# The final norm of a recurrent-mixer and mixture-of-experts layer: all rows normed under the last expert's down product, that expert's rows normed again and written by index

## What is computed

```python
def rms_norm(x, g):
    y = x * lax.rsqrt(jnp.mean(x * x, axis=-1, keepdims=True) + EPS)
    return y * g

def expert_choice_ffn(h, w_router, w_gate, w_up, w_down):
    cap = CAPACITY_FACTOR * n // N_EXPERTS            # 128 rows per expert
    aff = softmax(h @ w_router)
    gate, idx = lax.top_k(swapaxes(aff, 1, 2), cap)   # each expert picks its rows
    xg = h[idx]
    hid = silu(xg @ w_gate) * (xg @ w_up)
    y = (hid @ w_down) * gate[..., None]
    return zeros.at[idx].add(y)

x = x + mod[:, 2] * y_lat
h = modulate(rms_norm(x, norm_ffn_g), mod[:, 3], mod[:, 4])
x = x + mod[:, 5] * expert_choice_ffn(h, ...)
return rms_norm(x, final_g)
```

## Time and profile before

| what | us |
|---|---|
| median of three runs | 1784.28 |
| the profiled execution's own time | 1784.54 |
| its span (first to last record) | 1782.4 |
| own time less span | 2.14 |
| PE busy / DVE busy / ACT busy / POOL busy | 1610.7 / 1391.7 / 1222.2 / 213.3 |

### The profile page before, as it was taken

One profiled execution on the slowest core, in us unless ns is written; L12 is line 12 of the kernel. 1 busy time (PEld: TensorE's weight loads), 2 busy tenths in 40 slices (PEclk: granted clock), 3 DMA queues, 4 the chain that ended last, 5 costly groups with the idle time before them and its releaser, 6 DMA issues.

```text
span 1782.4 us, 21010 instructions
## 1 busy us (share of the span) xinstructions
PE 1610.7 (90%) x7524; PEld 1321.7 (74%) x7524; DVE 1391.7 (78%) x1044; ACT 1222.2 (69%) x1138; POOL 213.3 (12%) x129
## 2 busy tenths in 40 slices
PE   4999999997896049999999999999999999999992
PEld 1777777776785038888888888888888888888872
DVE  2677887789312958998988988988988988988982
ACT  3688788875324138787787787787787778777752
POOL 0400000003000500101101101011011011011010
PEclk6999999998997569999999999999999999999996
DMA  9223433434566039999999999999999999999945
GB/s 347 80 92 122 154 112 124 155 106 131 201 231 282 0 122 372 361 405 381 374 405 377 378 401 369 388 393 371 401 381 371 402 378 368 402 386 365 397 176 212
DMA packets 106448, 511.25 MB, mean 287 GB/s; under 512 B 10362, under 2 KB 36632, under 8 KB 55200
## 3 DMA queue, kind: packets, MB, share of 16 engines
q1 hardware_dynamic: 98912, 483.33, 69.7%
q0 software_dynamic: 7488, 27.27, 5.6%
HBM read 479.10 MB, written 31.46 MB: 286 GB/s over the span
## 4 chain that ended last, share of the span: by engine, by line
PE 84%; DVE 9%; ACT 3%; SPq 2%; DMA 1%; issue 1%; POOL 0%; ACTq 0%; DVEq 0%; POOLq 0%
PE psum L1281 13%; PE psum L1283 13%; PE psum L1289 13%; PE psum L1333 7%; PE psum L1335 7%; PE psum L1340 7%; PE psum L1082 5%; PE psum L1084 5%; PE psum L1083 5%; PE psum L1320 2%; PE psum L1190 2%; PE psum L1191 2%; PE psum L1192 2%; SPq L276 1%; DVE top_id L994 1%; DVE top_val L992 1%
## 5 line engine op out<-in xcount | busy, mean ns | idle before, releaser
L1007 DVE TENSOR_TENSOR part_l<-raw,part_h 128x2048 fp32r<-128x2048 f32 x378 | 844.0, 2285 | 71.6 <-ACT part_h L517 70.1
L517 ACT ACTIVATE part_h<-raw 128x2048 fp32r<-128x2048 f32 x384 | 720.8, 1917 | 158.1 <-PE psum L1289 82.4
L1281 PE MATMUL psum<-part_h,xgT_h 128*128 128x512 f32 x1024 | 284.5, 395 | 4.6 <-DVE xgT_l L1032 4.6
L1283 PE MATMUL psum<-part_h,xgT_l 128*128 128x512 f32 x1024 | 280.0, 390 | 0.0
L1289 PE MATMUL psum<-part_l,xgT_h 128*128 128x512 f32 x1024 | 279.9, 390 | 0.0
L1283 PEld LDWEIGHTS psum<-part_h,xgT_l 128*128 128x128 f32 x1024 | 192.8, 188 | 40.8
L1289 PEld LDWEIGHTS psum<-part_l,xgT_h 128*128 128x128 f32 x1024 | 192.6, 188 | 40.7
L1281 PEld LDWEIGHTS psum<-part_h,xgT_h 128*128 128x128 f32 x1024 | 189.6, 189 | 41.7 <-DVE xgT_l L1032 5.0
L1333 PE MATMUL psum<-part_h,hidT_h 128*128 128x512 f32 x512 | 158.7, 391 | 1.4 <-DVE hidT_l L1019 1.4
L1335 PE MATMUL psum<-part_h,hidT_l 128*128 128x512 f32 x512 | 158.5, 391 | 0.0
L1340 PE MATMUL psum<-part_l,hidT_h 128*128 128x512 f32 x512 | 137.2, 390 | 0.0
(11 more groups left out here) (213 smaller groups left out, 2318.4 us busy)
## 6 DMA issues: line engine op xcount, KB each, us to landing
raw<-in_exp_w_gate_dram SPq DMA_DIRECT2D x128, 1024.0 KB, 6.7
raw<-in_exp_w_up_dram SPq DMA_DIRECT2D x128, 1024.0 KB, 6.3
raw<-in_exp_w_down_dram SPq DMA_DIRECT2D x128, 1024.0 KB, 8.7
ada_piece<-in_ada_w_dram SPq DMA_DIRECT2D x16, 1024.0 KB, 6.6
ada_buf<-in_ada_w_dram SPq DMA_DIRECT2D x8, 1024.0 KB, 12.9
u_raw<-in_a_w_in_dram SPq DMA_DIRECT2D x10, 512.0 KB, 3.8
g_raw<-in_a_w_in_dram SPq DMA_DIRECT2D x10, 512.0 KB, 8.6
y_scr<-y_h POOLq DMA_DIRECT2D x10, 512.0 KB, 3.8
```

Source lines behind the costliest of these rows:

```text
L517: return nc.scalar.activation(dst, src, ACT.Identity)
L1007: v.tensor_tensor(part_l[slot][:], raw[slot][:], part_h[high][:].bitcast(F32), ALU.subtract).then_inc(sem["part_l_ready"], 1)
L1281: mm(dst, xgT_h[slot][:, i, :], wh[:, f, :], start=(i == 0), stop=False)
L1283: mm(dst, xgT_l[slot][:, i, :], wh[:, f, :], start=False, stop=False)
```

## The change

All eight tiles of `x_scr` are loaded when the scatter of expert 14 (the last but one) has landed, into tiles `fin[t]` that lie in buffers free by then, tiles 3 to 7 also behind the use of up chunks u4 to u6 of the last expert. ACT squares them in three groups (tiles 0 to 2, 3 and 4, 5 to 7), the output of Square going to PSUM banks 0 to 3, with one Sqrt for a group, put between its splits: group 0 behind the split of d5, group 1 behind d6, group 2 behind d7. DVE scales group 0 in place between its splits of d6 and d7, groups 1 and 2 behind d7 and ahead of `expert_out(E - 1)`. SP stores each tile. `fin_g` is loaded behind the last weight chunk.

The last expert's scatter into `x_scr` is gone. Instead, POOL gathers its 128 rows of `x_scr` (with 15 experts added) into `x_last` (the buffer of `xg`) when scatter 14 has landed; at the end DVE adds them to `y_out`, ACT squares and takes the root, DVE takes the reciprocal and multiplies, and POOL writes the 128 rows to the output by index, once the stores of all eight tiles have landed.

```diff
@@ -158,10 +158,11 @@
     hidT_l = place("hidT_l", [P, FF // P, P], F32R, 184)
     y_out = place("y_out", [P, D], F32, 192)
 
-    fin_in = place("fin_in", [P, NT, D], F32, 0)
-    fin_out = place("fin_out", [P, NT, D], F32, 32)
-    fin_g = place("fin_g", [P, D], F32, 64)
-    fin_junk = place("fin_junk", [P, D], F32, 68)
+    fin_kb = [148, 152, 160] + [raw_kb[i // 2] + 4 * (i % 2) for i in range(NT - 3)]
+    fin = [place(f"fin{t}", [P, D], F32, kb) for t, kb in enumerate(fin_kb)]
+    fin_g = place("fin_g", [P, D], F32, 201)
+    x_last = xg
+
     assert base + (SM + 2.8125) * KB <= nc.sbuf_usable_end
 
     psum = nc.alloc_psum_tensor("psum", [P, 8, HALF], F32)
@@ -199,7 +200,7 @@
         id_ready first_id_ready gathered xg_turned xgT_ready xgT_h_ready xgT_l_ready part_h_ready part_l_ready
         chunk_used silu_done hid_ready hid_turned hidT_h_ready hidT_l_ready
         y_ready id2_ready scattered fin_g_loaded fin_sq fin_rms fin_rstd
-        fin_ready fin_stored bias_loaded""".split()
+        fin_ready fin_stored last_loaded last_step last_stored bias_loaded""".split()
     piece_loaded = [stack.enter_context(nc.semaphore(f"piece_loaded{i}")) for i in range(2)]
     raw_loaded = [stack.enter_context(nc.semaphore(f"raw_loaded{i}")) for i in range(NR)]
 
@@ -416,15 +417,15 @@
                 load_chunk(E - 1, "d", i)
 
 
-            sp.wait_ge(sem["chunk_used"], 3 * E * CHUNKS)
             sp.dma_start(fin_g[:], row_of(final_g)).then_inc(sem["fin_g_loaded"], 16)
-            sp.wait_ge(sem["scattered"], 16 * E)
+            sp.wait_ge(sem["scattered"], 16 * (E - 1))
             for t in range(NT):
-                sp.dma_start(fin_in[:, t, :], x_scr[t * P:(t + 1) * P, :]).then_inc(x_loaded[t], 16)
+                if t >= 3:
+                    sp.wait_ge(sem["chunk_used"], chunk(E - 1, "u", 4) + (t - 3) // 2 + 1)
+                sp.dma_start(fin[t][:], x_scr[t * P:(t + 1) * P, :]).then_inc(x_loaded[t], 16)
             for t in range(NT):
                 sp.wait_ge(sem["fin_ready"], t + 1)
-                sp.dma_start(out[0, t * P:(t + 1) * P, :], fin_out[:, t, :]).then_inc(sem["fin_stored"], 16)
-            sp.wait_ge(sem["fin_stored"], 16 * NT)
+                sp.dma_start(out[0, t * P:(t + 1) * P, :], fin[t][:]).then_inc(sem["fin_stored"], 16)
             for i in range(2):
                 sp.wait_ge(x2_stored[i], PER_SLOT)
                 sp.wait_ge(n_stored[i], PER_SLOT)
@@ -506,8 +507,15 @@
                 gather(e, sem["id_ready"], e)
                 scatter(e - 2, e - 1)
             scatter(E - 2, E - 1)
-            scatter(E - 1, E)
-            pool.wait_ge(sem["scattered"], 16 * E)
+            pool.wait_ge(sem["scattered"], 16 * (E - 1))
+            pool.wait_ge(sem["xg_turned"], 2 * E)
+            nc.gpsimd.indirect_dma_start(x_last[:], None, x_scr, bass.IndirectOffsetOnAxis(ap=id_gather[:, 0:1], axis=0)
+                                         ).then_inc(sem["last_loaded"], 16)
+            pool.wait_ge(sem["fin_stored"], 16 * NT)
+            pool.wait_ge(sem["last_step"], 4)
+            nc.gpsimd.indirect_dma_start(out[0], bass.IndirectOffsetOnAxis(ap=id_gather[:, 0:1], axis=0), y_out[:], None
+                                         ).then_inc(sem["last_stored"], 16)
+            pool.wait_ge(sem["last_stored"], 16)
             pool.wait_ge(sem["y_stored"], 32 * NB)
 
 
@@ -724,18 +732,34 @@
             with act.Fori(1, E // 2) as j:
                 expert(j * 2, 0)
                 expert(j * 2 + 1, 1)
+            groups_fin = ((0, 3), (3, 5), (5, NT))
+            junk_fin = [psum[:, 2 * s:2 * s + 2, :].rearrange("p b f -> p (b f)") for s in range(2)]
+
+            def squares(part):
+                lo, hi = groups_fin[part]
+                for t in range(lo, hi):
+                    act.wait_ge(x_loaded[t], 32)
+                    if t >= 2:
+                        act.wait_ge(sem["fin_sq"], t - 1)
+                    nc.scalar.activation(junk_fin[t % 2], fin[t][:], ACT.Square, accum_out=stat[:, 0, t:t + 1]).then_inc(sem["fin_sq"], 1)
+                act.wait_ge(sem["fin_sq"], hi)
+                nc.scalar.activation(stat[:, 1, lo:hi], stat[:, 0, lo:hi], ACT.Sqrt, scale=1.0 / D,
+                                     bias=eps[:]).then_inc(sem["fin_rms"], 1)
+
             for i in range(CHUNKS):
                 split(E - 1, "d", i)
                 if i == 4:
                     turn_hidden(E - 1)
-
-            act.wait_ge(sem["chunk_used"], 3 * E * CHUNKS)
-            for t in range(NT):
-                act.wait_ge(x_loaded[t], 32)
-                nc.scalar.activation(fin_junk[:], fin_in[:, t, :], ACT.Square, accum_out=stat[:, 0, t:t + 1]).then_inc(sem["fin_sq"], 1)
-                act.wait_ge(sem["fin_sq"], t + 1)
-                nc.scalar.activation(stat[:, 1, t:t + 1], stat[:, 0, t:t + 1], ACT.Sqrt, scale=1.0 / D,
-                                     bias=eps[:]).then_inc(sem["fin_rms"], 1)
+                elif i == 5:
+                    squares(0)
+                elif i == 6:
+                    squares(1)
+            squares(2)
+            act.wait_ge(sem["last_step"], 1)
+            nc.scalar.activation(junk_fin[0], y_out[:], ACT.Square, accum_out=stat[:, 0, NT:NT + 1]).then_inc(sem["fin_sq"], 1)
+            act.wait_ge(sem["fin_sq"], NT + 1)
+            nc.scalar.activation(stat[:, 1, NT:NT + 1], stat[:, 0, NT:NT + 1], ACT.Sqrt, scale=1.0 / D,
+                                 bias=eps[:]).then_inc(sem["last_step"], 1)
 
 
         @block.vector
@@ -1056,20 +1080,36 @@
             with dve.Fori(1, E // 2) as j:
                 expert(j * 2, 0)
                 expert(j * 2 + 1, 1)
+            groups_fin = ((0, 3), (3, 5), (5, NT))
+
+            def scaled(part):
+                lo, hi = groups_fin[part]
+                dve.wait_ge(sem["fin_rms"], part + 1)
+                v.reciprocal(stat[:, 0, lo:hi], stat[:, 1, lo:hi]).then_inc(sem["fin_rstd"], 1)
+                dve.wait_ge(sem["fin_rstd"], part + 1)
+                for t in range(lo, hi):
+                    v.scalar_tensor_tensor(fin[t][:], fin[t][:], stat[:, 0, t:t + 1], fin_g[:], ALU.mult, ALU.mult
+                                           ).then_inc(sem["fin_ready"], 1)
+
             for i in range(CHUNKS):
                 split(E - 1, "d", i)
                 if i == 4:
                     gate_up(E - 1)
                     turn_hidden(E - 1)
+                elif i == 6:
+                    dve.wait_ge(sem["fin_g_loaded"], 16)
+                    scaled(0)
+            scaled(1)
+            scaled(2)
             expert_out(E - 1)
-
-            dve.wait_ge(sem["fin_g_loaded"], 16)
-            for t in range(NT):
-                dve.wait_ge(sem["fin_rms"], t + 1)
-                v.reciprocal(stat[:, 0, t:t + 1], stat[:, 1, t:t + 1]).then_inc(sem["fin_rstd"], 1)
-                dve.wait_ge(sem["fin_rstd"], t + 1)
-                v.scalar_tensor_tensor(fin_out[:, t, :], fin_in[:, t, :], stat[:, 0, t:t + 1], fin_g[:], ALU.mult, ALU.mult
-                                       ).then_inc(sem["fin_ready"], 1)
+            dve.wait_ge(sem["y_ready"], 2 * E)
+            dve.wait_ge(sem["last_loaded"], 16)
+            v.tensor_tensor(y_out[:], y_out[:], x_last[:], ALU.add).then_inc(sem["last_step"], 1)
+            dve.wait_ge(sem["last_step"], 2)
+            v.reciprocal(stat[:, 0, NT:NT + 1], stat[:, 1, NT:NT + 1]).then_inc(sem["last_step"], 1)
+            dve.wait_ge(sem["last_step"], 3)
+            v.scalar_tensor_tensor(y_out[:], y_out[:], stat[:, 0, NT:NT + 1], fin_g[:], ALU.mult, ALU.mult
+                                   ).then_inc(sem["last_step"], 1)
 
 
         @block.tensor
```

## The result

Four runs of the changed kernel gave 1765.05 to 1766.59 us, median 1766.10, against 1784.99 for four runs of the kernel before: ratio 0.9893, 95% interval 0.988 to 0.9906. It is faster by 18.9 us. The forecast was a gain of 22.3 us and a time of 1762.0, within 1760.0 to 1765.5; the measured median lies 0.6 above the range. The direction was right, the size was not.

A forecast was written before the change was run, and what follows sets the result against it. PE bounds the kernel until 1749.50, followed by an uncovered tail: 31.45 us removed from 1750.95 on, 9.15 added, 22.3 saved, span 1760.1. Forecast median 1762.0 us, range 1760.0 to 1765.5.

The forecast's parts named there:

- To the span's end 0.3: Last term of the added tail: 0.3 us from the landing of the write by index to the span's end, at 1760.1.
- Cover: Under the last down product: squares and scaling fit in idle ACT and DVE; DVE ends at 1748.8, margin 0.7 us.
- POOL's start: In the tail, from DVE's last multiply to POOL's write: 0.2 us taken, with 0.1 to 0.8 kept as bounds.
- The write by index: Landing of POOL's final write: 4.2 us, taken from the indirect gather, between a plain store 2.6 and accumulating scatter 6.4.
- The gather of `x_last`: Behind scatter 14: issued about 1715.3, landed by 1727, read by DVE at 1751; no cost, 24 us of cover.
- starved gather of the shared-port rule: Rival: gather descriptors starve until DVE idles, at worst 1748.8, landing at 1753.0: 1764.2 us; chance 0.04.
- Table load: In ACT's group 0: one load of 1.28 us, none in the tail; the skill's figure would add 0.7 us.
- Stores: Tile stores at the end: last issued at 1748.8, no queue, landed at 1751.4, at 6.2 us landing by 1755.0.
- Their rival: The last stores, not the multiply, release the final write: 1762.6, or 1764.6 with a burst of five; chance 0.06.
- The slower rival: Squares wait on a late tile 2 ahead of ACT's split d6, stalling PE; chance 0.02, half of it slower.
- change of sign: In the slower rival: the gain turns to loss where tile 2 lands at 1759; at 1762 the time is 1787.
- the limit that this pricing sets: In the slower rival: ACT must start group 0, 5.0 us long, by 1737; every us later costs one more.

The follow-up runs named there:

- the changed kernel's second profile: The changed kernel run again unaltered, in a second group of four runs: median 1765.01 us, from 1764.41 to 1765.86.
- the kernel whose norm is not covered: Against the changed kernel, the eight tiles' squares and scaling moved behind the last down chunk, loads and write by index left in place: median 1776.04 us.
- the run with late loads: Against the changed kernel, SP holds back the eight tile loads until PE has used down chunk d2: median 1777.15 us.
- the two whose SP waits: The changed kernel with the wait for the last write moved from POOL to SP, median 1762.58 us; the same with the last rows' chain in halves, 1762.77.

## Why the prediction was wrong

The mechanism was right, and one term of its sum was mis-sized: the step **"To the span's end 0.3"**. I took that from the kernel before, where SP came last, and carried it over to an end at which POOL comes last. It measured 3.6, of which 3.18 is POOL's DRAIN. That DRAIN is the cause: one more wait on POOL brought 3.3 us of tail into the old kernel, and moving the last wait to SP took 1.8 us out of the new one. The row stood in the trace of before, at 1758.6, but the busy view leaves such instructions out, and none of the rows that the prediction works with shows it.

By the prediction's own steps, each in the profiled execution:

| step | forecast | measured |
|---|---|---|
| ACT: split d6 starts | 1731.4 | 1731.28 |
| DVE: group 2 ends | 1748.8 | 1747.90 |
| `y_out` starts | 1749.53 | 1749.53 |
| last multiply ends | 1755.4 | 1755.23 |
| POOL's write is issued | 1755.6 | 1756.03 |
| its landing takes | 4.2 | 3.4 |
| landing to the span's end | 0.3 | 3.6 |
| span | 1760.1 | 1763.0 |

- **Cover**: right. The squares into PSUM took 1.00 to 1.03, below the 1.04 of rows 6. One started 1.04 behind another; only the last of a group, with its Sqrt behind it, took 1.15 to 1.17. Three scalings took 3.67, not 3.85. The prediction misread one thing here without harm: it has ACT and DVE idle from 1730 on, but they still worked 3.65 and 2.29 us between 1730 and 1735 in the kernel before. Its own sum of the two queues does count those splits.
- **POOL's start**: 0.8 after DVE's multiply. I took only the 0.19 ahead of the DMA; the chain shows 0.54 "issue" before that, and the old kernel had 0.50 there, between the copy and the DMA. It is just at my bound of 0.8.
- **The write by index**: 3.4, half way between the plain store of 2.6 and the gather of 4.2. I had taken the latter.
- **The gather of `x_last`**: issued at 1714.88, POOL time 1.09, landed in 7.6, 28 us early. The starved gather of the shared-port rule did not happen. This execution says little of the rule, since DVE was idle from 1715.09 to 1715.52. In the changed kernel's second profile the gather started at 1716.82, under a DVE operation that ended at 1718.88; it took 2.94 us of POOL and landed in 10.0, still 25 us early. So in these profiles a running DVE operation delays it by up to 1.9 us, and it does not wait for DVE's first long idle time. The page that the prediction names (the Trainium skill, SBUF — State Buffer, section "SBUF: two separate sides") spells out the starved descriptors for DVE's 2-port modes; for two SBUF inputs it names the lock, and only against a GpSimd operation that reads SBUF.
- **Table load**: 1.28 at 1729.78 with Sqrt 0.01 behind it, none in the tail. The further 1.38 of drain in the Trainium skill (ScalarE: Activation LUTs, section "What ACT_TABLE_LOAD costs") is not in this trace either.
- **Stores**: landed in 2.6 to 2.8, no queue. Their rival came true only in the kernel whose norm is not covered, where the scaling is late.
- **The slower rival**: its mechanism is real, its price was too low. It charges a late tile only from the point where PE stalls, 10.6 us on, and puts the change of sign at a tile 2 that lands at 1759. In the run with late loads (tile 2 read at 1743.19) group 0 ended at 1745.95, 4 us past the limit that this pricing sets, and `y_out` started 12.85 us later. With the margin of 1.6 and one for one behind it, the gain of 18.9 us would be gone with a tile 2 at about 1749, by an estimate from its square at 1728.63 in the changed kernel. The prediction also gives "slower" a chance of 0.02, twice what its list of rivals leaves for it.

The 2.9 us of the span are -0.2 + 0.6 - 0.8 + 3.3. The rest of the miss against the median is 1.2: the profiled execution was put 0.26 above the median and came out 1.05 below it, as the fastest of its four, less the 0.1 by which the time around the span was shorter. The other group of four gave 1765.01, inside the range. That would have been luck: the missing 3.3 was the same there, and a short landing and the spread of the medians would have hidden it. The direction was right; the range was too narrow, since its upper end held only costs of steps that I had listed, and the end of the program was not among them. The best kernels measured are the two whose SP waits, 22.4 and 22.5 us below the kernel before, which can't be told apart.

## What to carry to other kernels

When a change makes another engine the last to finish, price that engine's own end: look at the queue rows (q) of the closing line, not only in the busy view. Here, let SP hold the last wait, with its DRAIN of 7 ns, and let POOL run into its DRAIN while its DMA is under way: 1.8 us for one line. And work put into an idle stretch needs two numbers: how late it may end (1.6 us on DVE) and what stands behind it in its queue (the split of d6 on ACT, which held PE up for 3.5 us when tile 2 came late, and all of DVE's scaling, which held `y_out` up for 12.9).

## What the runs showed of the hardware that was not expected

- The DRAIN that closes POOL's program takes 3.09 to 3.18 us with nothing in flight, 5.01 when started with the write by index (two profiles) and 7.86 when started with the accumulating scatter (one), ending 1.7 and 1.6 us after the landing.
- A plain write of 128 rows of 4 KB by index lands in 3.3 to 3.4 us and occupies POOL for 0.99; the accumulating scatter of as many rows takes 6.2 to 6.4 and 1.56. Both with nothing else in flight.
- The gather of `x_last`, started under most of a DVE operation with two SBUF inputs, took POOL 2.94 us and landed in 10.0 (one profile). Where DVE was idle at its start or within 0.2 us of it, it took 1.00 to 1.09 and landed in 7.5 to 7.8 beside the tile loads, in 4.7 where those came late.
- A pause of 3.5 us on PE was followed by over 4 us at a granted clock of 0.50, the lower of its two levels.
